# Windows and memory attention of a hybrid decoder step written out slot by slot, with the weighting of three patterns in the output stage, two tiles at the head of the projection, and the last tile in halves

## The reference, cut to what matters

```python
DILATED_PATTERNS = ((128, 1), (512, 4), (2048, 16))   # (window, stride): 128 keys each
proj = rmsnorm(x, norm_in) @ w_in
cq, ckv, kr, qb, kb, vb, qc, gate = jnp.split(proj, SPLIT_POINTS, axis=-1)

def masked_softmax_stats(s, mask):
    s = jnp.where(mask, s.astype(jnp.float32), -jnp.inf)
    m = jnp.max(s, axis=-1, keepdims=True)
    e = jnp.exp(s - m)
    l = jnp.sum(e, axis=-1, keepdims=True)
    return e / l, (m + jnp.log(l))[..., 0]

def cross_attend(q, mk, mv):
    s = jnp.einsum('bshd,bmhd->bhsm', q, mk) * ATT_SCALE
    p = jax.nn.softmax(s.astype(jnp.float32), axis=-1).astype(mv.dtype)
    return jnp.einsum('bhsm,bmhd->bshd', p, mv)

# output: o = [latent 512 | windows 256 | memory 256]
y = rmsnorm(x + (o * jax.nn.silu(gate)) @ w_out, final_gain)
```

## Time and profile before

| | |
|---|---|
| median of 3 runs | 2078.2 us (2067.97 to 2080.51) |
| profiled execution | 2075.85 us, of which the span of the trace is 2074.2 |
| granted clock of TensorE, mean | 0.972 |
| busy PE / DVE / ACT / POOL | 93% / 52% / 45% / 20% of the span |
| projection, windows and memory, output | 391, 242, 402 us |

### The profile page before, as it was taken

One profiled execution on the slowest core, in us unless ns is written; L12 is line 12 of the kernel. 1 busy time (PEld: TensorE's weight loads), 2 busy tenths in 40 slices (PEclk: granted clock), 3 DMA queues, 4 the chain that ended last, 5 costly groups with the idle time before them and its releaser, 6 DMA issues. The chain is left out here.

```text
span 2074.2 us, 47175 instructions
## 1 busy us (share of the span) xinstructions
PE 1934.3 (93%) x17532; PEld 1468.7 (71%) x17532; DVE 1080.4 (52%) x3163; ACT 932.6 (45%) x2106; POOL 425.2 (20%) x584
## 2 busy tenths in 40 slices
PE   6999999788877989999999989999999989999997
PEld 5888888466655876667666656666666668888886
DVE  4334242476795447767776645555555753232332
ACT  4333332377863225556555634444444543333332
POOL 0111111233463313113311142222222200000000
PEclk9999999897999999999999999999999989999999
DMA  8333333442356552011201189877875452332331
GB/s 293 101 114 100 114 100 94 120 155 92 120 147 162 145 168 88 21 45 43 65 17 25 47 258 287 245 227 231 230 223 196 127 206 83 110 91 81 98 101 44
DMA packets 178426, 270.37 MB, mean 130 GB/s; under 512 B 28088, under 2 KB 138632, under 8 KB 169336
## 3 DMA queue, kind: packets, MB, share of 16 engines
q1 hardware_dynamic: 158456, 169.74, 28.8%
q0 software_dynamic: 19808, 98.40, 14.0%
HBM read 213.06 MB, written 54.76 MB: 129 GB/s over the span
## 5 line engine op out<-in xcount | busy, mean ns | idle before, releaser
L75 PE MATMUL proj_acc<-proj_w_hi,proj_x_hi 128*128 128x512 f32 (+2 forms) x544 | 197.7, 363 | 19.0 <-DVE proj_x_lo L299 12.4
L76 PE MATMUL proj_acc<-proj_w_lo,proj_x_hi 128*128 128x512 f32 (+2 forms) x544 | 196.1, 360 | 0.0
L77 PE MATMUL proj_acc<-proj_w_hi,proj_x_lo 128*128 128x512 f32 (+2 forms) x544 | 195.7, 360 | 0.0
L1660 ACT ACTIVATE mla_probs<-mla_probs,mla_bias 128x256 f32<-128x256 f32 (+15 forms) x128 | 153.0, 1196 | 11.6 <-DVE mla_bias L1724 7.3
L1720 DVE CUSTOM_DVE_ANT_0 mla_probs<-mla_scores,mla_zero 128x512 f32<-128x512 f32 x192 | 124.7, 687 | 59.1 <-PE mla_scores L1576 58.8
L75 PEld LDWEIGHTS proj_acc<-proj_w_hi,proj_x_hi 128*128 128x128 f32 x544 | 104.1, 191 | 32.3 <-DVE proj_x_lo L299 12.4
L818 ACT ACTIVATE win_probs<-win_probs,win_bias 128x256 f32<-128x256 f32 (+1 forms) x256 | 117.4, 462 | 17.9 <-DVE win_bias L857 17.6
L2045 PE MATMUL dec_scores<-dec_keysT,sample_q_lat 128*64 128x512 f32 x512 | 122.7, 600 | 2.2 <-DVE dec_krT L2211 1.2
L353 DVE COPY proj_featT<-proj_tr 128x512 f32<-128x512 f32 x34 | 23.5, 691 | 188.1 <-PE proj_tr L406 186.4
L2233 DVE COPY dec_pT<-dec_p_turned 128x256 f32<-128x256 f32 x80 | 33.9, 424 | 157.7 <-PE dec_outs L2061 129.7
L77 PEld LDWEIGHTS proj_acc<-proj_w_hi,proj_x_lo 128*128 128x128 f32 x544 | 103.8, 191 | 13.0
(11 more groups left out here) (407 smaller groups left out, 5003.9 us busy)
## 6 DMA issues: line engine op xcount, KB each, us to landing
win_v_tile<-wv_out SPq DMA_DIRECT2D x75, 128.0 KB
proj_x_raw<-in_xT SPq DMA_DIRECT2D x17, 512.0 KB, 6.2
proj_rows<-in_x SPq DMA_DIRECT2D x17, 512.0 KB, 5.3
featT<-proj_featT POOLq DMA_DIRECT2D x34, 256.0 KB, 2.8
late_ckv<-in_xT SPq DMA_DIRECT2D x17, 512.0 KB, 7.0
host_buf<-mix SPq DMA_DIRECT2D x17, 512.0 KB, 3.6
late_ckv<-in_x SPq DMA_DIRECT2D x17, 512.0 KB, 4.1
y_out<-host_buf POOLq DMA_DIRECT2D x17, 512.0 KB, 6.4
```

The lines of the kernel that those rows point to most:

```text
L75: pe.matmul(out, lh, rh, start=start, stop=False)
L76: pe.matmul(out, lh, rl, start=False, stop=False)
L77: return pe.matmul(out, ll, rh, start=False, stop=stop)
L1660: act.activation(row, row, ACT.Exp, bias=bias[:, at:at + 1], scale=-1.0, accum_out=total[:, at:at + 1]).then_inc(exp_done, 1)
```

## The change

**Windows and memory.** All 64 slots are written out on every engine. PE's order within a step t is now: scores of t, transposes of t-2, turning back of t-4, values of t-3. `probs` has three buffers, and each head's mask step releases its exponential, and that its transposes. DVE's mask step multiplies by the negative scale and takes the minimum, which is the exponential's bias as it stands. Memory and `d1` slots read queries and keys from `xT`, `qT` and `kT`, and POOL copies only for `d16` and `d4`. The copy `outT` alternates between ACT and DVE (all by DVE in `d16`). A result's buffer is one of six. The `d1` result is stored unweighted (`pat1`), and its maxima and sums stay in `ahead.stat`; those of the other two are loaded there at step 56, in pieces of 32 bytes. The identity matrix is one buffer for all stages.

**Weighting.** The shares of all tiles are worked out in one go at the start of `prompt_latent_projections`, by DVE and ACT, and stored (`shares`). In `output_projection` SP loads for each tile the three patterns, the shares and the remaining columns of `mix` in two pieces (six transfers for one), and POOL multiplies and adds (`merge`, 5 steps) ahead of the gating.

**Projection.** The first 416 columns of weight block 0 and x of tile 0 come first; raw weights pass through five buffers (the memory tokens' buffers lent). Tile 1's first two chunks are multiplied together with tile 0's, two weight blocks behind, into `mem_acc`; its other two chunks follow. The third group of transposes has a bank of its own (`three`).

**Last tile.** Squares, norm and store go in halves, and SP issues the stores.

```diff
+        w_from = [w_raw[:, r, :] for r in range(RAW)] + [t[:].rearrange("p a b -> p (a b)")[:, 0:W_COLS] for t in (memT, mem_rows)]
+        RING = len(w_from)
...
+        three = [tr[:, 0, :, :], tr[:, 1, :, :], mem_acc[:, 1, :].rearrange("p (j t) -> p j t", t=P)]
...
+            sp.dma_start(w_from[0][:, 0:HEAD], io["w_in"][0:P, 0:HEAD]).then_inc(head_loaded, 16)
+            load_early(0, x_first)
             load_weights(0)
...
+            load_weights(1)
+            load_early(1, x_second)
...
-            by_chunk = 3
+            by_chunk, behind = 1, 2
             for k in range(DK - by_chunk):
-                pe.wait_ge(w_low, k + 1)
                 for c in range(NC):
-                    first(c, k)
...
+                if k >= behind:
+                    if k == behind:
+                        pe.wait_ge(x_low, 4)
+                    for c in range(MT):
+                        first(1, c, k - behind)
...
+            for c in range(MT):
+                for k in range(DK - by_chunk - behind, DK):
+                    mm = first(1, c, k)
+                mm.then_inc(proj_done, 1)
+            project(1, 1, 2)
+            project(1, 1, 3)
+            transposes(0, 0, into=two, free=(1, 2, 3))
+            tile(2, 0, after_early=True)
...
+    NBUF, NREC, NPROBS, PART = 4, 6, 3, SEQ // 4
+    SEGS = ("mem", "d16", "d4", "d1")
...
+    LAG_BACK, DRAIN = 3, 5
+    out_on_act = [g % 2 == 0 and SLOTS[g][0] != 'd16' for g in range(NG)]
...
+            def load_values(g):
+                v = g - NT_PROMPT
+                if v >= NBUF:
+                    sp.wait_ge(out_done, g - NBUF + 1)
+                n = blocks_of(g)
+                for j in range(n):
+                    sp.dma_start(v_tile[:, v % NBUF, 2 - n + j, :], token_rows(io["wv_out"], g, n - 1 - j)).then_inc(v_loaded[v % NBUF], 32 // n)
...
+            def store(g):
+                seg, w = SLOTS[g]
+                sp.wait_ge(result_done, g + 1)
+                if seg == "mem":
+                    sp.dma_start(io["mix"][w * P:(w + 1) * P, MIX_A + 256:], rec[:, g % NREC, 0:256]).then_inc(stored[g % NREC], 16)
+                elif seg == "d1":
+                    sp.dma_start(io["pat1"][w * P:(w + 1) * P, 0:256], rec[:, g % NREC, 0:256]).then_inc(stored[g % NREC], 16)
+                else:
+                    sp.dma_start(token_rows(io["pat16" if seg == "d16" else "pat4"], g), rec[:, g % NREC, :]).then_inc(stored[g % NREC], 16)
...
+            for t in range(NG + LAG_BACK + 1):
+                if t < NT_PROMPT:
+                    load_ahead(t)
+                if NT_PROMPT <= t + 2 < NG:
+                    load_values(t + 2)
+                if t >= LAG_BACK + 1:
+                    store(t - LAG_BACK - 1)
+                if t == 3 * NT_PROMPT + NBUF + NBUF:
+                    stored_by(3 * NT_PROMPT)
+                    for k, name in ((1, "pat16"), (2, "pat4")):
+                        sp.dma_start(ahead.stat[:, :, k, :], io[name].rearrange("(w p) c -> p w c", p=P)[:, :, 256:]).then_inc(ahead.stat_loaded, 16)
+            stored_by(NG)
...
+                for h in range(H_B):
+                    rows = slice(HD * (h % 2), HD * (h % 2) + HD)
+                    if seg == "mem":
+                        mine, keys = xT[rows, h // 2, w * P:(w + 1) * P], mkT[rows, h // 2, :]
+                    elif seg == "d1":
+                        mine, keys = qT[rows, h // 2, w * P:(w + 1) * P], kT[rows, h // 2, (w - n + 1) * P:(w + 1) * P]
+                    else:
+                        s = staged_at[g] % 2
+                        mine, keys = q_tile[rows, s, h // 2, :], k_tile[rows, s, h // 2, (2 - n) * P:]
...
+                pe.wait_ge(turned_dve, g)
+                for h in range(H_B):
+                    pe.wait_ge(exp_done, H_B * g + h + 1)
+                    for j in range(2 - n, 2):
+                        for lane in range(2):
+                            rows = slice(HD * lane, HD * lane + HD)
+                            mm = pe.transpose(turned[:, lane, h, j, :], probs[rows, g % NPROBS, h, j * P:(j + 1) * P], ident[rows, rows])
...
+            for t in range(NG + DRAIN):
+                if t < NG:
+                    score(t)
+                if 0 <= t - 2 < NG:
+                    turn(t - 2)
+                if 0 <= t - 4 < NG:
+                    turn_back(t - 4)
+                if 0 <= t - 3 < NG:
+                    value(t - 3)
...
+                    act.wait_ge(masked, H_B * g + h + 1)
+                    pr = probs[:, g % NPROBS, h, (2 - n) * P:]
+                    act.activation(pr, pr, ACT.Exp, bias=low[:, h:h + 1], scale=-1.0, accum_out=total[:, h:h + 1]).then_inc(exp_done, 1)
...
+            for t in range(NG + DRAIN):
+                if t < NG:
+                    exponentials(t)
+                if 0 <= t - 1 < NG:
+                    keep_turned(t - 1)
+                if 0 <= t - 2 < NG:
+                    keep_out_rows(t - 2)
...
+            def keep_scores(g):
...
+                if g >= NPROBS:
+                    dve.wait_ge(turned_done, g - NPROBS + 1)
+                if g >= NREC and seg != "d1":
+                    dve.wait_ge(stored[g % NREC], 16 * (g // NREC))
...
+                add = zero[:].broadcast_to([P, 2 * P]) if seg == "mem" else mask[:]
+                for h in range(H_B):
+                    dve.tensor_tensor_reduce(probs[:, g % NPROBS, h, (2 - n) * P:], scores[:, u, h % 2, h // 2, (2 - n) * P:],
+                                             add[:, (2 - n) * P:], -ATT_SCALE, -LOWEST, ALU.add, ALU.min, low[:, h:h + 1]).then_inc(masked, 1)
...
+            def result(g):
...
+                dve.wait_ge(back_done, g + 1)
+                if SLOTS[g][0] == "d1" and g >= NREC:
+                    dve.wait_ge(stored[r], 16 * (g // NREC))
+                dve.tensor_copy(rec[:, r, 0:256], back[:, 0:256]).then_inc(result_done, 1)
+
+            for t in range(NG + DRAIN):
+                if t < NG:
+                    keep_scores(t)
+                if 0 <= t - 1 < NG:
+                    keep_turned(t - 1)
+                if 0 <= t - 3 < NG:
+                    result(t - 3)
+                if 0 <= t - 2 < NG:
+                    keep_out_rows(t - 2)
...
+            def load_mix(t):
+                sp.dma_start(mix[:, OWN], io["pat1"][t, :]).then_inc(pats_loaded, 16)
+                for k, name in enumerate(("pat16", "pat4")):
+                    sp.dma_start(pats[:, k, :], io[name][t, 0:256]).then_inc(pats_loaded, 16)
+                sp.dma_start(shares[:].rearrange("p g c -> p (g c)"), io["shares"][t, :]).then_inc(pats_loaded, 16)
+                for cols in (slice(0, OWN.start), slice(OWN.stop, D)):
+                    sp.dma_start(mix[:, cols], io["mix"][t, cols]).then_inc(mix_loaded, 16)
...
+            for c, cols in enumerate(HALVES):
+                sp.wait_ge(normed, LAST + 3 + c)
+                sp.dma_start(io["y_out"][LAST * P:NT * P, cols], out[:, cols]).then_inc(last_stored, 16)
+            sp.wait_ge(last_stored, 32)
...
+            def merge(n):
+                pool.wait_ge(pats_loaded, n * 64 + 64)
+                by_head = lambda ap: ap.rearrange("p (h d) -> p h d", d=HD)
+                for k, mine in enumerate((mix[:, OWN], pats[:, 0, :], pats[:, 1, :])):
+                    pool.tensor_tensor(by_head(mine), by_head(mine), shares[:, k, 0:H_B].rearrange("p (h o) -> p h o", o=1).broadcast_to([P, H_B, HD]),
+                                       ALU.mult).then_inc(pats_scaled, 1)
+                pool.wait_ge(pats_scaled, n * 3 + 3)
+                pool.tensor_tensor(mix[:, OWN], mix[:, OWN], pats[:, 0, :], ALU.add).then_inc(pats_added, 1)
+                pool.wait_ge(pats_added, n * 2 + 1)
+                pool.tensor_tensor(mix[:, OWN], mix[:, OWN], pats[:, 1, :], ALU.add).then_inc(pats_added, 1)
...
+            merge(0)
+            merge(1)
+            with pool.Fori(0, LAST - 2) as n:
+                merge(n + 2)
+                store(n)
...
+                    dve.wait_ge(mix_loaded, n * 32 + (16 if last else 32))
+                    dve.wait_ge(pats_added, n * 2 + 2 if not last else 2 * LAST)
```

More of the change, by code:

```diff
@@ L2564, in slot @@
                     dve.wait_ge(out_free, n)
[L2565 removed]
+                    for cols in HALVES if not split else [slice(0, D)]:
+                        dve.scalar_tensor_tensor(out[:, cols], rows[:, w, cols], r[:, w:w + 1], f_gain[:, cols], ALU.mult, ALU.mult).then_inc(normed, 1)
             run(dve, slot, split_out)
```

705 lines of the change are left out of this document (328 added, 377 removed).

## The result

| | before | after |
|---|---|---|
| median, us | 2076.9 (4 runs) | 2015.3 (4 runs, 2013.1 to 2020.0) |
| ratio | | 0.970, 95% interval 0.968 to 0.972 |
| profiled execution: time, span, granted clock | 2075.85, 2074.2, 0.972 | 2013.11, 2011.5, 0.982 |

The account below looks back on a forecast made before the run. PE was taken as the bound, with windows-stage waits for ACT and POOL to remove. Terms -48.8, -10, -5.2, -2.8, -0.5 and +1.0 gave -66.3: profiled 2009.5, median 2012 us; 8-in-10 range 1995 to 2031.

Parts of the forecast that it names:

- Slots: Windows and memory stage: long slots 3.2 us (PE), short 2.35 (DVE), stage 193.3 against 242.1, so -48.8 us.
- The reason given for it: Windows stage: ACT's exponentials come late (20.4 us of PE waits) because probabilities have two buffers and heads are released together.
- Tight only in short ones: Windows stage: a result's store, with six buffers, may press DVE's mask step, due after 2.8 us in short slots, 3.6 in long.
- Combination at nothing: Output stage: POOL's merging, 3.5 us a tile, and SP's added loads are hidden and cost nothing; 56 us without cover.
- Shares: Windows stage, from slot 59: loading 4096 rows of 32 bytes takes 8 us; costs nothing, at worst 8.
- Two tiles early: Projection's head: tile 2 starts at 55.4 us against 64.97; taken as -10, bounds -5 and -13.
- The third bank: Projection: a bank of its own for the third group of transposes removes its waits, -5.2 us.
- Last tile: End of the output stage: 4.6 us from DVE's end instead of 7.2; -2.8, bounds -1 and -5.
- A: Windows stage: latencies between engines keep today's slots of 3.5 and 2.56 us; 2029 us; 0.17 together with B.
- B: Windows stage: the clock falls in short slots, up to +17 us, 2029; 0.17 together with A.
- C: Windows stage: all of it at 1.2 GHz, +111 us, 2172; 0.02 together with other losses over 1%.
- D: Windows stage: fetching written-out code costs PE +10 us, 2022; inside the forecast range given 0.76.

Follow-up runs that it names:

- e7: e1 with eight result buffers in the windows stage instead of six; 2000.8 us.
- e3: Kernel after with the slot order of before (transposes one step behind the scores, values and turning back two), three probability buffers kept; 2050.0 us.
- e2: Kernel after without POOL's weighting and adding of the patterns in the output stage (it only signals); 2017.0 us.
- e1: Kernel after with the buffer `shares` allocated behind the output stage's operands instead of ahead of them; 2007.6 us.
- e11: Kernel before with 32 bytes allocated ahead of `x_hi` in its output stage; 2078.0 us, ratio 1.002.
- e8: Kernel after with the projection's third group of transposes back in the first of two banks; 2027.9 us.
- e6: Kernel before with the changed kernel's input projection alone; 2062.2 us, ratio 0.993.
- e10: e7 with both operands of the projection moved to 256 bytes above a multiple of 512; 1991.8 us.
- e9: e7 with 96 bytes ahead of `x_raw`, putting the projection's loaded operand at 224 above a multiple of 512; 1997.2 us.

## Why the prediction was right

The time was right, and the signs of the terms behind it were, with one term missing. By its own steps:

- **Slots.** The mechanism held: PE sets the pace of the long slots, at 2.95 where I took 3.2. "So PE's own work is 3.2" was 0.25 too much, and not because of other gaps in that slot; there were none. I took off the idle time of 0.36, and the slot became 0.57 shorter: the wait had also taken the overlap with the matmul ahead and made the transposes 0.05 longer, as at the bank of the projection; the rest I put down to the new order. For the short slots PE's 2.06 was right: they take 2.05 once the stores are out of the way (e7), and DVE has hardly a gap in them, so my 2.35 for DVE was too much. The stage came out 185.5, 7.8 below the forecast. My base of 242.1 was some 7 longer than in two other executions, by the clock in stride 16. The two errors cancel, which is why -48.8 meets the measured -49.5. That is luck in the sum, not in the mechanism.
- **The reason given for it** is in part unproven. The waits for exponentials fell from 20.4 us to waits of 8.1 on ACT, and e7 removes most of these; whether the transposes' extra step or the release by head, the third buffer and the lost bias did it, no run separates. What e3 does show is what the depth is needed for at the turning back, where DVE has half of the copies.
- **"Tight only in short ones."** The store behind six result buffers made DVE wait 10.7 us, and cost 7.8 to 9.5 us of the stage (e7). And it wasn't tight only in short slots: three of the 13 waits, 1.5 us, lie in stride 16, eight, 6.0 us, in long slots of stride 4, and two, 3.2 us, in memory slots. It was seen and not priced; within the undershoot above it didn't show.
- **Combination at nothing.** Right for POOL (e2): its rows give 0.63 to 0.79 us a step, 3.5 us a tile as forecast, hidden. I asked only who waits for whom. The new tile `shares` moved every operand allocated behind it, and that cost 7.5 us (e1; 6.6 for e11's 32 bytes), a term that the sum put at nothing. No rival had it; 2012 was met since other terms came out better.
- **Shares.** The 64 KB transfers of 32-byte rows landed in 4.4 us, inside the 8 allowed, and no value load came late. By the mean rate of that stretch, 148 GB/s, 64 KB would be 0.4 us. The stores of 128 KB beside them landed in 2.8, so small rows took longer for half the bytes. The Trainium skill names a fixed overhead for each packet ("DMA: Bandwidth & Descriptors", "Why small descriptors are slow (HBM only)"). The trace agrees in direction; how much of the 4.4 us is by packet, no run separates.
- **Two tiles early.** -7.5 for -10 in the profiled pair: tile 2 at 57.4, since PE still waited for weights at the head, 2.4 us before the second chunk and 0.8 later; in the fastest head of the other runs (e8, 55.25) it is -9.7.
- **The third bank.** -8.4 for -5.2, and e8 gives all of it to the bank. The term was sized by the idle time alone; a tile loses 0.57 us by a wait of 0.35. The sum of both, -15.9, is e6's -16.4, and -15.2 was forecast.
- **Last tile.** -2.6 for -2.8; 4.3 from DVE's end for 4.6.
- **Rivals.** A (slots at 3.5) didn't happen. B and C didn't: the granted clock is 0.95 in the memory segment and 1.00 after. D didn't, as far as this trace shows: PE's waits put to issue are 0.6 us in the stage, 2.0 before.

## What to carry to other kernels

A new small tile ahead of others in an allocation is an edit to all of them: compare the durations of untouched matmuls before and after, and put new tiles last. Price a wait of PE from start to start of its matmuls, with and without it, and not by the idle time that the profile gives: here 0.35 us of idle stood for 0.57. Compare a stretch in which PE waits for no load (here from tile 2 to the memory tokens' product, the same to 0.01 us in eight executions) before calling an edit without effect. Check a stage that is to be shortened in a second execution, or in any variant that leaves it alone, before its time becomes the base of a sum. After a pipeline is deepened, look for what is now next: two more result buffers were worth 7.8 to 9.5 us of the stage. The lowest median (e10: shares last, eight buffers, projection's operands moved) is 1991.8 us, by the ratios (0.961 and 0.970) 0.99 of the kernel after; e7 and e9 can't be told from it.

## What the runs showed of the hardware

A product of 512 columns in fp32 took 0.389 us with the loaded operand's start 256 bytes above a multiple of 512 in its partition, and 0.394 to 0.397 at 288, 320 and 352; from start to start 0.2265 and 0.2335 us. The order of instructions, the clock (1.00 between the stage's first and last tiles) and the streamed operand's start were the same, and within one stage products whose loaded tile had not moved kept 0.389 to 0.390. It made the output stage 6.6 to 8.4 us of 366 longer. The load itself took 0.187 to 0.189 us in all of these runs; only the product's step grew. On that load the Trainium skill ("TensorE: Matmul & The Clock Gate", "Step-by-step: what each phase is for") says that it takes no read bandwidth from the running matmul. The page says nothing of where the operand starts; here that changes the step by 3%, and why stays open. Which multiple is wanted in the output stage (128, 256 or 512, or agreement of both operands) stays open too.

In the projection the streamed blocks start at 224, 352, 480 and 96 above a multiple of 512 in turn. From tile 2 to the memory tokens' product it took 298.2 us with the loaded operand at 128, 295.8 at 160, 297.6 at 224, and 297.5 with the loaded operand and the first streamed block at 256. No rule tried gives this order.

A wait of PE costs more than its idle time, since matmuls overlap: transposes start 0.11 us apart and take 0.27; a wait of 0.35 between two of them made it 0.62.
